# Three edits to a hybrid RWKV-7 / GLA / mixture-of-experts step: an output projection taken in quarters, a routing by comparisons, and transfers of the experts put in another order

## The reference, cut to what matters

```python
h = rmsnorm(x, norm1_g) * (1 + sc1) + sh1
proj = h @ w_in
y_r, shift, wkv = rwkv7_group(proj[:, :1664], ...)      # 8 heads x 64, one state per head, step by step in time
y_g, gla        = gla_group(proj[:, 1664:], ...)        # 4 heads, key 64, value 128
x = x + gt1 * (concat(y_r, y_g) @ w_out)
h = rmsnorm(x, norm2_g) * (1 + sc2) + sh2
lg = h @ w_router_group + b; gi = argmax(lg)            # one of 4 groups
le = (h @ w_router_expert + b)[4 experts of group gi]
top_v, top_i = top_k(softmax(le), 2)                    # two of its experts
wts = softmax(lg)[gi] * top_v / sum(top_v)
out = sum over the two of wts * (silu(h @ gate_e) * (h @ up_e)) @ down_e    # D 1024, inner 512, 16 experts
x = x + gt2 * out
y = rmsnorm(x, normf_g) * (1 + scf) + shf
```

## Time and profile before

| | |
|---|---|
| device time, median of 3 runs | 1731.43 us (1724.76 to 1734.33) |
| the profiled execution's own time | 1728.46 us |
| its span | 1726.1 us |
| TensorE (PE) busy | 1541.3 us, 89% |
| VectorE (DVE) / ScalarE (ACT) / GpSimd (POOL) busy | 535.1 / 380.5 / 175.9 us |
| mean granted clock of TensorE | 0.938 of full |
| weight loads of the experts' block | 20 each of gate, up and down, 2048 KB each |
| last overflow product ends, next block begins | 1651.50, 1660.6 us |

### The profile page before, as it was taken

How to read it: one execution, slowest core, us unless ns; L and a number is a source line. 1 busy time by engine, 2 the same in 40 slices (tenths; PEclk the granted TensorE clock), 3 DMA queues, 4 the chain that set the end, 5 groups by cost and what they waited for, 6 DMA issues and landing times. The chain is left out here.

```text
span 1726.1 us, 30030 instructions
## 1 busy us (share of the span) xinstructions
PE 1541.3 (89%) x12659; PEld 1114.5 (65%) x12659; DVE 535.1 (31%) x997; ACT 380.5 (22%) x784; POOL 175.9 (10%) x272
## 2 busy tenths in 40 slices
PE   4899999999948999999999997479999999999555
PEld 3566666566627787677768763468787887868321
DVE  4255464502104544454445342411000000000018
ACT  5332133202113232233223221011101111110023
POOL 0011111100012111011101100010000000000030
PEclk9899999999978999999999996579999999999778
DMA  8336654522137213212321200897878787794855
GB/s 305 107 121 230 218 195 148 181 76 76 63 100 252 63 39 99 87 45 68 99 62 39 68 32 6 316 384 286 299 248 307 262 298 268 266 318 176 296 220 218
DMA packets 180785, 299.53 MB, mean 174 GB/s; under 512 B 19184, under 2 KB 91182, under 8 KB 180656
## 3 DMA queue, kind: packets, MB, share of 16 engines
q1 hardware_dynamic: 163552, 240.96, 40.7%
q0 software_dynamic: 12928, 42.79, 6.4%
q10 hardware_dynamic: 4176, 13.90, 2.1%
HBM read 241.96 MB, written 55.64 MB: 172 GB/s over the span
## 5 line engine op out<-in xcount | busy, mean ns | idle before, releaser
L2048 PE MATMUL banks<-moe_xT,moe_wg 128*128 128x160 f32 x1024 | 148.4, 304 | 0.8 <-issue 0.8
L2048 PEld LDWEIGHTS banks<-moe_xT,moe_wg 128*128 128x128 f32 x1024 | 142.8, 193 | 7.8 <-issue 7.8
L2048 PE MATMUL banks<-moe_xT,moe_wu 128*128 128x160 f32 x1024 | 144.3, 299 | 0.0
L2048 PEld LDWEIGHTS banks<-moe_xT,moe_wu 128*128 128x128 f32 x1024 | 140.8, 190 | 0.0
L1215 PE MATMUL banks<-mixer_w_out,mixer_yT 128*128 128x512 f32 (+1 forms) x288 | 127.3, 600 | 4.5 <-DVE mixer_yT L1661 3.7
L598 PE MATMUL banks<-xT,w_v 128*128 128x352 f32 (+1 forms) x384 | 118.7, 469 | 0.0
L598 PE MATMUL banks<-xT,w_r 128*128 128x352 f32 (+1 forms) x384 | 118.6, 469 | 0.0
L598 PE MATMUL banks<-xT,w_k 128*128 128x352 f32 (+1 forms) x384 | 118.3, 468 | 0.0
L1471 POOL TENSOR_TENSOR mixer_LTm<-mixer_LT,level 128x256 f32<-128x256 f32 (+1 forms) x90 | 72.2, 825 | 407.9 <-ACT mixer_LTo L1527 282.7
L2089 PE MATMUL banks<-moe_wd,moe_hid 128*128 128x512 f32 x256 | 112.5, 592 | 0.0
L598 PEld LDWEIGHTS banks<-xT,w_v 128*128 128x128 f32 x384 | 72.6, 190 | 45.2 <-issue 2.2
(11 more groups left out here) (434 smaller groups left out, 2070.3 us busy)
## 6 DMA issues: line engine op xcount, KB each, us to landing
moe_wg<-w_expert_gate SPq DMA_DIRECT2D x20, 2048.0 KB, 9.3
moe_wu<-w_expert_up SPq DMA_DIRECT2D x20, 2048.0 KB, 11.9
moe_wd<-w_expert_down SPq DMA_DIRECT2D x20, 2048.0 KB, 10.2
w_mod<-w_ada SPq DMA_DIRECT2D x8, 2048.0 KB, 7.4
mixer_feats<-feature_major SPq DMA_DIRECT2D x16, 768.0 KB, 8.2
wada<-w_ada SPq DMA_DIRECT2D x4, 2048.0 KB, 19.6
w_mod<-w_ada_final SPq DMA_DIRECT2D x4, 2048.0 KB, 8.2
mixer_feats<-feature_major SPq DMA_DIRECT2D x8, 1024.0 KB, 6.4
```

Source lines behind the costliest of these rows:

```text
L2048: mm = pe.matmul(bank[:, i * S_STATIC:(i + 1) * S_STATIC], wt[:, u, q, (t0 + i) * P:(t0 + i + 1) * P], xT[:, e % 2, q, :], start=q == 0, s ...
```

## The change

1. **Recurrence.** In the last front (`last`, the 64-token tile) the four quarters of the last full tile's projection leave the place (5, 1): `wo0a` comes after the G products, `wo0b` after SA, `wo1a` after the front, `wo1b` between `gvar` and `var` of the 64-token tile. They use banks 4 and 5. Adds, norm, transposes and router product of the full tile come behind the 64-token tile's projection on TensorE and ahead of its adds on VectorE. The 64-token tile's yT has a place of its own in `feats[1]`. `store(8)` goes behind the states on SyncE.
2. **Routing.** Places within a group of four are found by comparing each pair with a difference (`places`), for groups and for experts, on logits rather than on probabilities; `either` comes first, a running sum over tiles is made by four shifted additions, and ranks and counts are three products. Constants come from GpSimd. The softmaxes and shares are taken behind `plan_token`. `at_pos` is made in three parts, and lies in the buffer xT.
3. **Transfers.** Set 1 waits until the first two gathers have landed; zeros and last-norm rows stand ahead of set 5; the loop of overflow passes stands ahead of the last two tails.

```diff
@@ recurrence, TensorE
+            def back(n0, nm, m, late=False):
                             if late:
+                                w(pe, ("TI1_made", "TT1_made")[half], back.xx + half)
-                            mm = pe.matmul(psum[6 + half][0:m, :], yT[:, q, 0:m], w_out[...]
+                            mm = pe.matmul(psum[(4 if late else 6) + half][0:m, :], (yT_last if n0 == NT else yT)[:, q, 0:m], w_out[...]
+                last = not m_next
+                        if last and name in ("wo0a", "wo0b", "wo1a", "wo1b"):
+                            continue
@@ after the G products
                 if m_next:
                     start()
-                for name in ("ht0", "ht1"):
-                    if name in bk:
-                        bk[name]()
+                    for name in ("ht0", "ht1"):
+                        if name in bk:
+                            bk[name]()
+                else:
+                    bk["wo0a"]()
@@ after the SA products
-                if "rt" in bk:
-                    bk["rt"]()
                 if m_next:
+                    if "rt" in bk:
+                        bk["rt"]()
                     swap()
+                else:
+                    bk["wo0b"]()
@@ after front(8)
+            ahead, bk = back(8, None, P, True), back(9, None, DEC)
+            ahead["wo1a"]()
             turn_state(1)
-            for name in ("mu", "gvar", "var", "wo0a", "wo0b", "wo1a", "wo1b", "ht0", "ht1", "rt"):
+            for name in ("mu", "gvar"):
+                bk[name]()
+            ahead["wo1b"]()
+            for name in ("var", "wo0a", "wo0b", "wo1a", "wo1b"):
+                bk[name]()
+            for name in ("ht0", "ht1", "rt"):
+                ahead[name]()
+            for name in ("ht0", "ht1", "rt"):
                 bk[name]()
@@ ScalarE, after front(8)
-            for stage in (yc, gvar, var, norm):
+            for stage in (yc, gvar, var, ahead_norm):
                 stage()
+            norm()
+            ahead_ht(0)
+            ahead_ht(1)
             ht(0)
             ht(1)
@@ VectorE, after front(8)
             for stage in (mu, yg, yr):
                 stage()
+            ahead_add(0)
+            ahead_add(1)
+            ahead_norm()
             add(0)
             add(1)
             norm()
+            ahead_rt()
             rt()
@@ experts, SyncE
             for s in range(NE + 2):
-                if s == 2:
+                if s == 1:
+                    for u in range(2):
+                        sp.wait_ge(sg(f"x{u}_loaded"), 16)
+                if s == 5:
                     sp.wait_ge(sg("zero_made"), 1)
                     ...
-            tail_out(O_SET)
-            tail_out(O_SET + 1)
             passes(sp, step)
+            tail_out(O_SET)
+            tail_out(O_SET + 1)
@@ experts, GpSimd
+            nc.gpsimd.iota(earlier_i[:, :, :], [[1, 4], [-1, 4]], base=0, channel_multiplier=0)...
+            nc.gpsimd.tensor_scalar(earlier[:, :, :], earlier_i[:, :, :], 0.0, -1e-37, ALU.is_gt, ALU.mult)...
+            for v in (either, sum1, sum2):
+                nc.gpsimd.memset(v[:, 0:PAD, :], 0.0)...
             (iotas; then count, token and the three offsets, made here and no longer on VectorE)
-                if i == main_tile(3):
+                if i == main_tile(9):
@@ experts, TensorE
+            pe.matmul(psum[0][:, 0:NT * NE], after[:, :], flat(either, PAD), start=True, stop=False)
+            pe.wait_ge(sg("summed"), 1)
+            pe.matmul(psum[1][:, 0:NE], ones[:, :], sum2[:, PAD + NP, :], start=True, stop=True)...
+            pe.matmul(psum[0][:, 0:NT * NE], ones[:, :], flat(sum2, PAD - 1), start=False, stop=True)...
+            pe.wait_ge(sg("tiles_hot"), 1)
             for n in range(NT):
+                pe.wait_ge(sg("pos_hot"), n // 3 + 1)
@@ experts, VectorE
+            def places(v):
+                then(V.tensor_tensor(ahead, v.unsqueeze(2).to_broadcast(E44), v.unsqueeze(3).to_broadcast(E44), ALU.subtract))
+                then(V.tensor_tensor(beats, ahead, earlier.unsqueeze(1).to_broadcast(E44), ALU.is_gt))
+                then(reduce(place4, beats, ALU.add))
+            places(logits[:, :, 0:NG])
+            then(V.tensor_scalar(group, place4, 0.0, None, ALU.is_equal))
+            then(V.memset(group[DEC:P, NP, :], 0.0))
+            (logits of the group into le, as before)
+            places(le[:, :, :])
+            then(V.tensor_scalar(top2, place4, 1.5, None, ALU.is_lt))
+            V.tensor_tensor(grouped(either[:, PAD:, :]), by_group(group), by_member(top2), ALU.mult)...
+            for out, v, by in ((sum1, either, 1), (sum2, sum1, 2), (sum1, sum2, 4)):
+                then(V.tensor_tensor(out[:, PAD:, :], v[:, PAD:, :], v[:, PAD - by:PAD - by + NT, :], ALU.add))
+            V.tensor_tensor(sum2[:, PAD:, :], sum1[:, PAD:, :], sum1[:, 0:NT, :], ALU.add)...
+            (picked and chosen: four steps)
+            then(V.tensor_scalar(over_i, psum[1][:, 0:NE], float(S_OVER - 1 - S_STATIC), 0.0, ALU.add, ALU.max))
+            then(V.tensor_scalar(nblk_i, over_i, 6, None, ALU.logical_shift_right))
+            then(V.tensor_copy(nblk, nblk_i))
+            then(V.tensor_tensor_scan(end, ones[:, 0:NE], nblk, 0.0, ALU.mult, ALU.add))
+            (start, over_by, slots: as before; tile_i and pos_i are compared as integers)
+            (at_tile, its product with token, then at_pos in three parts)
+            (plan_token; behind it the two softmaxes, shares and block numbers)
-                if e == 1:
+                if e == 6:
                     dve.wait_ge(sg("rows_loaded"), 112)
```

More of the change, by code:

```diff
@@ L1268, in front @@
                 back.xx = 6 * n + (6 if m == P else 5)
-                bk = back(n0, None, P) if not (isinstance(n, int) and n == 0) else {}
+                last = not m_next
+                bk = back(n0, None, P, last) if n else {}
                 start, swap = first_level(n + 1, 1 - u, m_next, n2) if m_next else (None, None)
@@ L1358, in front @@
                 w(pe, "ATT0_read", n1)
-                w(pe, "gated0", n0)
+                w(pe, "gated0", n0 if m_next else n0 - 1)
                 for h in range(8):
@@ L1579, in front @@
                     x6()
-                first or norm()
+                if not first and m_next:
+                    norm()
                 if m == P:
@@ L1586, in front @@
                     lt(n + 1, m_next, n1, n2)
-                first or ht(0)
-                first or ht(1)
+                if not first and m_next:
+                    ht(0)
+                    ht(1)
                 take(psum[6][0:m, :], SA[0:m, :], "SA", "Y_done")
@@ L1641, in back @@
                 F = feats[1 - u]
+                out = yT_last if n == NT else yT
                 def mu():
@@ L1756, in front @@
                 update(5)
-                first or add(0)
-                first or add(1)
-                first or norm()
+                if not first and m_next:
+                    add(0)
+                    add(1)
+                    norm()
                 w(dve, "U_done", n1)
@@ L1768, in front @@
                     start(n + 1, m_next, n1, n2)
-                first or rt()
+                if not first and m_next:
+                    rt()
                 if m_next:
@@ L2293, in _ @@
-            then(V.tensor_tensor(either[:, :, :], chosen[:, :, 0, :], chosen[:, :, 1, :], ALU.add))
-            V.memset(either[DEC:P, NP, :], 0.0).then_inc(sg("either_made"), 1)
-            then(V.tensor_tensor(emax[:, :], v1[:, :], v2[:, :], ALU.add))
-            then(V.reciprocal(emax[:, :], emax[:, :]))
-            then(V.tensor_tensor(pg[:, :], pg[:, :], emax[:, :], ALU.mult))
-            for i, v in enumerate((v1, v2)):
-                V.tensor_tensor(share[:, :, i], pg[:, :], v[:, :], ALU.mult)
-                then(V.tensor_copy(value[:, :, i], token[:, :]))
@@ new lines, in _ @@
+            dve.wait_ge(sg("ex_made"), 1)
+            then(reduce(pg[:, :], ex[:, :, :], ALU.add))
+            dve.wait_ge(sg("ex_made"), 2)
+            then(reduce(emax[:, :], prob[:, :, :], ALU.add))
+            for v in (pg, emax):
+                then(V.reciprocal(v[:, :], v[:, :]))
+            then(V.tensor_tensor(prob[:, :, :], prob[:, :, :], wide(emax[:, :], E4), ALU.mult))
+            for i, v in enumerate((v1, v2)):
+                then(V.tensor_tensor(taken4[:, :, :], prob[:, :, :], picked[i][:, :, :], ALU.mult))
+                then(reduce(v[:, :], taken4[:, :, :], ALU.add))
@@ L2352, in _ @@
+            then(V.tensor_tensor(emax[:, :], v1[:, :], v2[:, :], ALU.add))
+            then(V.reciprocal(emax[:, :], emax[:, :]))
+            then(V.tensor_tensor(pg[:, :], pg[:, :], emax[:, :], ALU.mult))
+            for i, v in enumerate((v1, v2)):
+                then(V.tensor_tensor(share[:, :, i], pg[:, :], v[:, :], ALU.mult))
             then(V.tensor_tensor(ended[:, :, :], end[:, :].unsqueeze(1).to_broadcast([P, NBO, NE]),
```

184 lines of the change are left out of this document (95 added, 89 removed).

## The result

| | before | after |
|---|---|---|
| median | 1729.49 us (1724.76 to 1734.33, 4 runs) | 1672.72 us (1670.46 to 1677.46, 4 runs) |
| profiled execution, its span | 1728.46, 1726.1 us | 1674.74, 1672.5 us |
| mean granted clock | 0.938 | 0.952 |
| TensorE busy | 1541.3 us | 1524.3 us |

The ratio is 0.9675 with a 95% interval of 0.9638 to 0.9713: 56.8 us less. The forecast was 1670 (1654 to 1691). Run again later as e11_again the kernel took 1672.17 (1668.37 to 1677.77, 5 runs).

What follows compares the result with a forecast made beforehand. TensorE bounds the kernel except in the recurrence's last chain, the routing up to the first expert product, and the loop's overflow pass. Gains 14.9 + 2.5 + 12.7 + 6.2 + 22.7 = 59.0 us gave 1670 us, range 1654 to 1691.

Steps and rivals of the forecast that it cites:

- 1, recurrence's end: 64-token tile's chain: norm wait, transposes and router product leave, quarters fill in, clock stays full; net 14.9 us gained.
- the long wait: TensorE's 2.31 us wait for the full tile's norm, in the small tile's chain; the clock's fall was put to it.
- 2, end of the block: Logits to the next block's first transfer: states go out earlier, ahead of store(8); 2.5 us gained (0 to 3).
- 3, routing: Experts' block start to first gather's issue: 23.1 us instead of 35.8; 12.7 gained (10.5 to 13.5).
- 4, plan to product: First gather to first expert product: gather lands in 4.2 us, product 9.0 after issue; 6.2 gained (2 to 7).
- 5, overflow pass: Overflow pass in the loop: weights arrive before TensorE asks, 25.0 instead of 47.7 us; 22.7 gained (15 to 24).
- 6, zeros and rows: Zeros and final rows moved from expert 2's to expert 5's loads: cost 0, with 15 us of slack.
- B: Rival: the loop's overflow pass is not freed, something else is late there; 1681 to 1692 us, chance 0.12.
- C: Rival: the clock stays at half in the small tile's chain; 1678 to 1690 us, chance 0.12.
- D: Rival: the zero block delays experts 5 to 7 by 5 to 15 us; 1675 to 1685 us, chance 0.06.
- E: Rival: zeros and rows make gate 5 so late that the kernel is slower than before; chance 0.02.
- F: Rival: the change fails on two of five terms, no pass gain and no clock; 1695 to 1720 us, chance 0.02.

Runs made afterwards that it cites:

- e11_again: The changed kernel run once more, unchanged, beside the loop that ends at n: 1672.17 us, ratio 0.9658.
- e4: Changed kernel with the four quarters of the full tile's projection back at (5, 1), in one piece ahead of the chain: 1680.82 us, ratio 0.9721.
- e1: Kernel before with only the recurrence's part of the change: 1714.42 us, ratio 0.9907.
- e5: Changed kernel without the hold of set 1, so expert 1's weights go right behind expert 0's: 1674.17 us, ratio 0.9679.
- e3: Kernel before with only the transfers' part of the change: 1703.94 us, ratio 0.9861.
- e6: Changed kernel with the last two tails again ahead of the loop of overflow passes on SyncE: 1694.43 us, ratio 0.9791.
- e7: Changed kernel with zeros and last-norm rows back ahead of set 2, the hold of set 1 kept: 1681.69 us, ratio 0.9709.
- e10: Changed kernel with the overflow loop running to n and ScalarE copying the full tile's transposes ahead of the small tile's norm: 1668.54 us, ratio 0.9643.
- e11: The changed kernel run once more, unchanged: 1672.17 us, ratio 0.9658.
- e8: Changed kernel with one edit, the loop of overflow passes running to n instead of testing each turn: 1670.50 us, ratio 0.9646.

## Why the prediction was right, point by point

The time came out 2.7 us above the forecast. The five terms with a gain came out at 57.3 instead of 59.0. The clock at the first expert product gave 2.4 us more, which was luck (see below), and in the profiled execution the stages that did not change took 6.1 back.

**1, recurrence's end: 14.9 forecast, 13.5 measured** (14.6 less 1.1). The sum is nearly right, with terms wrong in it that nearly cancel, which is luck. That the clock would not fall without the long wait was wrong: it fell twice in the chain, and the two quarters cost 1.5 and 1.8 us more than 3.6. e4 shows that it falls without the wait, with no quarter in the chain. On the other side I had taken no gain for the SA and SU products and 1.0 for Y. These rows of the kernel before stand against those of after (timeline):

```profile
1031.65 1.96 PE L1389 MATMUL banks<-mixer_Gn,mixer_TTx 64*64 64x64 f32 x16
...
1041.37 0.69 PE L1420 MATMUL banks<-mixer_feats,mixer_Ss 128*128 128x64 f32 x2
...
1046.36 1.06 PE L1430 MATMUL banks<-ident,mixer_S 128*64 128x128 f32 x4
```

Y took 4.99 us there and 3.00 after (1028.83 to 1031.83): 2.0 instead of 1.0. SA and SU gave 0.8 each and the turned states 0.4. That is 3.0 more than forecast, against 3.3 lost in the quarters. The 1.5 us for three reads of a bank that the quarters hide was too much: TensorE waited for such a read once in the kernel before, 0.87 us ahead of the last variance product, and once in e4, at the same place; ahead of SA, SU and Y neither shows a wait. 0.9 of the 1.5 is there. The tail cost 1.1 instead of 0.5: the full tile's router product took 2.42 us (the forecast had 1.9) and ended 0.9 us after h2 (1070.67 against 1069.77). With ScalarE's copies ahead of the norm stage c was 25.33, the lowest of the profiles that have the edit (25.93 to 26.63 in the others), but that is one profile.

**2, end of the block: 2.5 and 2.1.** The states went out from 1055.67, inside the small tile's projection, and 1.78 us lie between logits and load. e1 has the 1.78 too; the order of the stores was not tried by itself.

**3, routing: 12.7 and 13.4.** Every version with the edit has 22.41 to 22.43 us, none of the others anything but 35.8. The steps came out within 0.7 us of the count: first placing 0.6 (0.7 forecast), `either` issued 4.1, `end` at 7.4, mask thirds 2.69 together, gather 22.4 (23.1). The scan took 0.19, the lower end. The range's reserve of 1.5 us for steps stretched by GpSimd was not needed: two-input steps of VectorE took 0.31 us both while GpSimd worked beside them and after. The cast that had taken 0.94 us is made by GpSimd now, so what stretched it stays open. By the Trainium skill (SBUF - State Buffer, on the shared port pair) a VectorE instruction with two SBUF inputs stands behind a GpSimd instruction that reads SBUF. The first placing, where the prediction looked for this, is no test of it: beside its rows at 1076.69 and 1077.04 GpSimd ran only memsets and iotas. The second placing is one: its subtract at 1078.88 began 0.04 us after a tensor_scalar of GpSimd (1078.84) and took the same 0.31 us. Nothing of the rule shows there, and the measurement decides, though it is a single pair of rows and overlaps by only 0.16 us.

**4, plan to product: 6.2 and 5.8.** The gather took 4.7 us and not 4.2, product 9.4 after its issue (9.0). e5 shows that the hold is 3.3 of it, and e3 that the term is there without the other edits (9.59).

**5, overflow pass: 22.7 and 22.5.** As forecast in each step. e6 shows the cause alone.

**6, zeros and rows: 0 and 0.** No wait for a weight appears. The rates were 391 to 418 GB/s, and the row of before with zeros among the traffic gave 406. e7 gives what the slack was worth.

**Not forecast.** The first expert product at full clock, 2.4 us. It is not the change's to keep: e3, with a gather as quick, has 6.58 us for it, e10 6.08, and e11, the same kernel as the changed one (timeline), 6.83; the changed kernel's own profile and those of e4 to e8 have it at 4.58.

```profile
1103.90 6.83 PE L2103 MATMUL banks<-moe_xT,moe_wg 128*128 128x160 f32 x32 [0.83 <-issue]
```

Also not forecast were stages a and j, 4.4 and 1.6 us to the bad, within what twelve profiles show for the same instructions. Of the dip in slices 13 and 14 of the page, the 6 is the stretch from 500 to 525 us, where TensorE was busy for only 3.30 us with its clock at 0.50, before the change as after. The 8 comes from this window of the changed kernel (the kernel before has 1.00 in it):

```profile
550.00:575.00 25.00, 24.06 (x298) 21.79 (x295) 11.59 (x23) 8.68 (x21) 6.65 (x8) 0.80 0.12 35
```

In e11 the same window has 0.80 too, and its stage a is 4.4 us shorter, so that this dip is not what the 4.4 us are. What they are stays open.

**The rivals.** B (pass not freed): no. C (clock half in the chain): in part; it fell twice, but cost 3.3 us and not 8 to 20. D, E (zeros): no such wait. F: no term was missing.

## What to carry to other kernels

When a queue issues in order, look for small transfers that wait for the last results and stand ahead of large ones that could start: swapping two lines was 22.5 of these 57 us. Work that must be done anyway was worth 5.4 us more between the steps of a serial chain than ahead of it, and only 0.9 of that was a wait covered: the rest came from TensorE's clock, which was back at full by the end of each wide product placed there. Look for the waits in a profile before counting on hiding them. A large transfer that is free in one place costs 9 us in another; when a stage ahead of it gets shorter, its place has to be looked at again.

## What the runs showed of the hardware that was not expected

- The clock fell with TensorE shown busy and no wait of over 0.9 us around it (e4: 1.00 to 0.50 at about 1025.7 us, among products of 64 and 128 columns, 5.5 us after 32 instructions of 512 columns), and it rose again during instructions of 512 columns in the changed kernel. It was low in one or both of the same two quarters in all eight profiles of the spread chain: `wo0a` took 4.8 to 6.5 us in every one, `wo1a` 3.70 in one and 5.2 to 5.5 in seven, the other two 3.60 and 3.70 always. Where exactly it falls differs from one execution to the next, and is worth up to 3 us in the chain and 2 at the first expert product. The Trainium skill (TensorE: Matmul & The Clock Gate, on the HAM clock gate) ties a fall of the clock to TensorE idling; the rows of e4 show one with TensorE busy by the trace (11.00 of 11.00 us), and there the measurement decides.
- After a wait of 1.31 us the clock fell in one execution and not in another.
- Zeros, rows and weights together moved at 391 to 418 GB/s for 83 us, against 406 for weights and zeros before, and TensorE did not lose a microsecond in them.
- A gather of 512 KB lands 4.7 us after its issue in an empty queue (after), and TensorE waits 3.4 us longer for it beside one expert's loads (e5).
- Thirteen empty turns of a loop, a comparison and a branch on each engine, cost 4.2 us, 0.3 us each.
